# A third place for split weights beside three raw rooms, and a new table of VectorE's taps and modulation steps

## What is computed

```python
mod = c_act @ w_ada[l] + b_ada[l]
shift, scale, gate = jnp.split(mod, 3, axis=-1)
h = _rmsnorm(x, norm_g[l]) * (1.0 + scale[:, None, :]) + shift[:, None, :]
z = h @ w_in[l]
...
y = jnp.concatenate([o_fft, o_na, o_ret, o_cv], axis=-1) @ w_out[l]
x = x + gate[:, None, :] * y
```

## Time and profile before

| what | value |
|---|---|
| time, median of 3 executions | 2083.03 us (2081.29 to 2087.2) |
| the profiled execution's own time | 2087.8 us |
| its span in the profile | 2085.9 us |
| TensorE busy | 2037.2 us, 98% of the span |
| VectorE busy | 1750.0 us, 84% |
| ScalarE busy | 1196.9 us, 57% |
| granted TensorE clock, mean | 0.991 of full |

### The profile page before, as it was taken

The page is one execution under the profiler, slowest core; times in us unless marked ns, Lnnn a source line. Parts: engine busy times, 40 slices in busy tenths (PEclk is TensorE's granted clock), DMA queues, the critical chain, the costliest instruction groups (busy, mean ns, idle before and its releaser), DMA issues.

```text
span 2085.9 us, 42604 instructions
## 1 busy us (share of the span) xinstructions
PE 2037.2 (98%) x18977; PEld 1641.7 (79%) x18977; DVE 1750.0 (84%) x1662; ACT 1196.9 (57%) x1079; POOL 57.0 (3%) x72
## 2 busy tenths in 40 slices
PE   8999999999999999999999999999999999999998
PEld 7889888888889955555556568888888888888887
DVE  7785687998887788999999999989877789898755
ACT  5553644454444578887877864456554454555543
POOL 0002300000000000000000000010000000100000
PEclk9999999999999999999999999999999999999999
DMA  8854577789888878999999987765758776557552
GB/s 302 298 202 165 180 289 271 287 293 329 317 319 300 298 300 343 420 420 420 420 420 413 416 320 277 257 197 190 282 189 302 270 290 245 194 197 275 200 202 102
DMA packets 96742, 595.27 MB, mean 285 GB/s; under 512 B 11176, under 2 KB 11336, under 8 KB 37808
## 3 DMA queue, kind: packets, MB, share of 16 engines
q1 hardware_dynamic: 94912, 583.66, 74.6%
q0 software_dynamic: 1648, 8.90, 1.2%
HBM read 588.32 MB, written 2.10 MB: 283 GB/s over the span
## 4 chain that ended last, share of the span: by engine, by line
PE 73%; DVE 13%; DMA 8%; ACT 3%; issue 2%; DVEq 0%; POOL 0%; ACTq 0%; POOLq 0%
PE GB L2256 54%; PE GB L2685 6%; DVE w_lo L1303 5%; PE MB L2685 4%; DVE W L1303 3%; DMA raw<-w_up 2%; ACT w_hi L653 2%; DMA Z<-w_ada 2%; DMA W<-w_ada 2%; DMA raw<-w_down 1%; DVE W L1274 1%; DMA raw<-w_gate 1%; DVE Z L1274 1%; PE MB L2843 1%; PE MB L2480 1%
## 5 line engine op out<-in xcount | busy, mean ns | idle before, releaser
L653 ACT ACTIVATE w_hi<-raw 128x2048 f16<-128x2048 f32 x308 | 588.1, 1910 | 697.2 <-PE GB L2256 673.6
L1303 DVE SCALAR_TENSOR_TENSOR w_lo<-raw,w_hi 128x2048 f16<-128x2048 f32 x308 | 706.1, 2294 | 236.8 <-ACT w_hi L653 235.5
L2256 PE MATMUL GB<-H,w_hi 128*128 128x256 f16 x4352 | 721.7, 274 | 16.5 <-DVE w_lo L1303 11.6
L2256 PE MATMUL GB<-H,w_lo 128*128 128x256 f16 x2176 | 595.4, 274 | 0.0
L2256 PEld LDWEIGHTS GB<-H,w_hi 128*128 128x128 f16 x4352 | 422.9, 98 | 82.8 <-DVE w_lo L1303 16.3
L2256 PEld LDWEIGHTS GB<-H,w_lo 128*128 128x128 f16 x2176 | 213.7, 98 | 25.4
L1274 DVE SCALAR_TENSOR_TENSOR W<-W,SM 128x1024 f32<-128x1024 f32 x150 | 192.2, 1281 | 35.6 <-DMA W<-w_ada 31.6
L2256 PE MATMUL GB<-w_hi,H 128*128 128x256 f16 x1280 | 210.8, 273 | 0.0
L2256 PE MATMUL GB<-w_lo,H 128*128 128x256 f16 x640 | 174.4, 273 | 0.0
L2256 PE MATMUL GB<-Z,w_hi 128*128 128x256 f16 x1024 | 170.0, 274 | 4.0 <-DVE w_lo L1303 4.0
L2256 PE MATMUL GB<-W,w_hi 128*128 128x256 f16 x1024 | 168.0, 273 | 1.8 <-DVE w_lo L1303 1.8
(11 more groups left out here) (487 smaller groups left out, 2751.2 us busy)
## 6 DMA issues: line engine op xcount, KB each, us to landing
raw<-w_in SPq DMA_DIRECT2D x144, 1024.0 KB, 5.4
W<-w_ada SPq DMA_DIRECT2D x160, 512.0 KB, 5.7
raw<-w_out SPq DMA_DIRECT2D x48, 1024.0 KB, 5.4
raw<-w_down SPq DMA_DIRECT2D x41, 1024.0 KB, 10.3
raw<-w_gate SPq DMA_DIRECT2D x34, 1024.0 KB, 11.7
raw<-w_up SPq DMA_DIRECT2D x32, 1024.0 KB, 12.8
raw<-xattn_wk SPq DMA_DIRECT2D x16, 1024.0 KB, 5.1
raw<-xattn_wq SPq DMA_DIRECT2D x16, 1024.0 KB, 7.6
```

What stands on the lines that cost most here:

```text
L653: act.activation(w, raw_at[r], ACT.Copy, scale=W_SCALE).then_inc(hi_done, 1)
L1303: dve.scalar_tensor_tensor(lo, raw_at[r], W_SCALE, hi, ALU.mult, ALU.subtract).then_inc(raw_taken[r], 1)
L2256: last = pe.matmul(o, a, m, start=first, stop=end and w_part is lo, skip_group_check=True)
```

## The change

Places: `SPL` is 3, and the third place for a high and a low half lies in raw room 3, which the projections no longer load into (three raw rooms). The experts use room 3 as a raw room from their fifth block on, as they keep their own places. `slot` turns the block's number so that the places meet at the borders of the experts' stretch. Waits follow: block m waits for block m - 3, the first expert load into room 3 waits for block 13 of `wo`, and the first block of `z0` waits until the experts gave room 3 up. `load_due(1)` lets the pieces of block m follow the load of block m + 1. The tables `TAPS_AT` and, for `z0` and `z1`, `ada_plan` are new: the sixteen early steps now end after block 11 and not 16, the sixteen late ones stand in pairs after blocks 38 to 42 and 45 to 47. The number of taps and steps is the same.

```diff
--- before.py
+++ after.py
@@ -22,7 +22,7 @@
 BLK = 2048
 RAW = 4
 ROOMS = RAW + 4
-SPL = 2
+SPL = 3
 IN_ORDER = [4, 5, 2, 3, 6, 7, 0, 1, 8, 9]
 POOL_AFTER = 38
 POOL_WINDOWS = (2, 4, 8, 16)
@@ -52,7 +52,7 @@
 GRID_W, NA_KW, NA_KH = 64, 16, 8
 REL_H, REL_W = 2 * NA_KH - 1, 2 * NA_KW - 1
 TAPS = 31
-TAPS_AT = {11: 5, 12: 4, 13: 6, 14: 4, 15: 6, 16: 4, 17: 6, 18: 6, 19: 6, 20: 6, 21: 6, 22: 2, 23: 6, 24: 6, 25: 2, 26: 6, 27: 6, 28: 2, 29: 4, 30: 6, 32: 6, 33: 2, 34: 6, 35: 2, 36: 3, 37: 2}
+TAPS_AT = {11: 5, 12: 6, 13: 6, 14: 6, 15: 6, 16: 6, 17: 6, 18: 6, 19: 6, 20: 6, 21: 2, 22: 6, 23: 6, 24: 2, 25: 5, 26: 6, 27: 2, 28: 1, 29: 6, 31: 6, 33: 6, 34: 1, 35: 5, 36: 4, 37: 3}
 DH = 64
 FOLD, MIRROR = P // 2, T // 2 + 1
 NEG = -1.0e30
@@ -120,9 +120,9 @@
     rooms, uses, last = [], [0] * ROOMS, [-1] * ROOMS
     for b in range(total):
         j = b - first
-        open_ = list(range(RAW))
+        open_ = list(range(RAW - 1))
         if 0 <= j < n:
-            open_ += [4] * (j >= 6) + [5] * (7 <= j < 126) + [6] * (j >= 7) + [7] * (13 <= j < 150)
+            open_ += [3] * (j >= 4) + [4] * (j >= 6) + [5] * (7 <= j < 126) + [6] * (j >= 7) + [7] * (13 <= j < 150)
         r = min(open_, key=lambda r: last[r])
         uses[r], last[r] = uses[r] + 1, b
         rooms.append((r, uses[r]))
@@ -142,9 +142,9 @@
         count[0] += 1
     short = [2, 2, 3, 3, *range(4, 16)]
     def halves(ph):
-        for m in [2, 2, 3, 4, 4, 5, 6, 6, 7, 8, 8, 9, 10, 12, 14, 16]:
+        for m in [2, 2, 3, 4, 4, 5, 6, 6, 7, 8, 8, 9, 9, 10, 10, 11]:
             put(ph, m)
-        for m in [35, 36, 37, 37, 38, 39, 39, 40, 41, 41, 42, 42, 43, 44, 45, 46]:
+        for m in [38, 38, 39, 39, 40, 40, 41, 41, 42, 42, 45, 45, 46, 46, 47, 47]:
             put(ph, m)
     for m in [2 + 2 * k // 3 for k in range(16)]:
         put("w_in", m)
@@ -212,8 +212,8 @@
         bank_free = [S(f"bank_free{j}") for j in range(4)]
 
         raw = sb("raw", [P, RAW, BLK])
-        w_hi = sb("w_hi", [P, SPL, BLK], F16)
-        w_lo = sb("w_lo", [P, SPL, BLK], F16)
+        w_hi = sb("w_hi", [P, 2, BLK], F16)
+        w_lo = sb("w_lo", [P, 2, BLK], F16)
         XT = sb("XT", [P, KC, T])
         H = sb("H", [P, 2 * BLK])
         xh = H[:, 0:BLK].bitcast(F16).rearrange("p (c t) -> p c t", t=T)
@@ -245,6 +245,14 @@
         HID = Zf[:, 8192:8192 + TILES * D_EXP].rearrange("p (k n) -> p k n", n=D_EXP)
         y_hi, y_lo = (Zf[:, k * 1024:(k + 1) * 1024].bitcast(F16).rearrange("p (k n) -> p k n", n=512) for k in range(2))
         hid_at = [H[:, k * 1024:(k + 1) * 1024] for k in range(4)] + [Zf[:, c * T:c * T + 1024] for c in (28, 48)] + [Yf[:, k * 1024:(k + 1) * 1024] for k in range(2)]
+        third = raw[:, RAW - 1, :].bitcast(F16)
+        hi_of = [w_hi[:, 0, :], w_hi[:, 1, :], third[:, 0:BLK]]
+        lo_of = [w_lo[:, 0, :], w_lo[:, 1, :], third[:, BLK:2 * BLK]]
+
+        def slot(s):
+
+            return (s + 2) % SPL
+
         raw_at = [raw[:, r, :] for r in range(RAW)] + [w3, Yf[:, 0:BLK], Yf[:, BLK:2 * BLK], Zf[:, 40 * T:48 * T]]
         hid_t = [a[:, 0:2 * ROWS_SORTED].bitcast(F16).rearrange("p (c n) -> p c n", n=ROWS_SORTED) for a in hid_at]
         slot_index = w2[:, 0:PLACES]
@@ -411,10 +419,10 @@
 
             return 2 + u if i == 0 and ph in K_MAJOR else 4 * i + 2 * u + 1
 
-        def done(eng, ph, j, i=0):
+        def done(eng, ph, j):
 
             s = where(ph, j)[1]
-            eng.wait_ge(block_done[s % SPL], s // SPL + 1 + 2 * i)
+            eng.wait_ge(block_done[s % SPL], s // SPL + 1)
 
         def pieces_in(eng, k):
 
@@ -456,6 +464,8 @@
                 r, n = rooms[where(ph, j)[0]]
                 if n > 1:
                     sp.wait_ge(raw_taken[r], n - 1)
+                elif r == RAW - 1:
+                    done(sp, "wo", 13)
                 elif r == 4:
                     sp.wait_ge(ada_mod, 7)
                 elif r in (5, 6):
@@ -495,7 +505,7 @@
                         m = 4 * k + j
                         load(ph, m, w[2 * n + j % 2, j // 2] if k == 0 and ph in K_MAJOR else w[2 * n + j // 2, j % 2])
                         due.append((ph, plan.get(ph, {}).get(m, [])))
-                        load_due(2)
+                        load_due(1)
                         if beside is not None:
                             beside(m)
 
@@ -636,20 +646,22 @@
                     act.wait_ge(raw_full[r], 16 * n)
                     act.wait_ge(block_done[s % SPL], s // SPL)
                 cut = slice(half * BLK // 2, half * BLK // 2 + BLK // 2)
-                act.activation(w_hi[:, s % SPL, cut], raw_at[r][:, cut], ACT.Copy, scale=W_SCALE).then_inc(hi_done, 1)
+                act.activation(hi_of[slot(s)][:, cut], raw_at[r][:, cut], ACT.Copy, scale=W_SCALE).then_inc(hi_done, 1)
 
             def split(ph, j, i=0):
                 b, s = where(ph, j)
                 r, n = rooms[b]
                 act.wait_ge(raw_full[r], 16 * n)
                 if ph == "moe":
-                    act.wait_ge(block_done[s % SPL], s // SPL - 1)
+                    act.wait_ge(block_done[(s - 4) % SPL], (s - 4) // SPL + 1)
                     if j < 2:
                         act.wait_ge(S("x_o"), 2 * X_HEADS)
                     w = ring_hi[j // 2 % 2][:, j % 2 * BLK:j % 2 * BLK + BLK]
                 else:
-                    act.wait_ge(block_done[s % SPL], s // SPL + 2 * i)
-                    w = w_hi[:, s % SPL, :]
+                    act.wait_ge(block_done[s % SPL], s // SPL)
+                    if (ph, j) == ("z0", 0):
+                        given_up(act, RAW - 1)
+                    w = hi_of[slot(s)]
                 act.activation(w, raw_at[r], ACT.Copy, scale=W_SCALE).then_inc(hi_done, 1)
                 if (ph, j) in parts_due:
                     ada_high(parts_due[ph, j])
@@ -1289,14 +1301,14 @@
                 b, s = where(ph, j)
                 dve.wait_ge(hi_done, s + 1 + half)
                 cut = slice(half * BLK // 2, half * BLK // 2 + BLK // 2)
-                ins = dve.scalar_tensor_tensor(w_lo[:, s % SPL, cut], raw_at[rooms[b][0]][:, cut], W_SCALE, w_hi[:, s % SPL, cut], ALU.mult, ALU.subtract)
+                ins = dve.scalar_tensor_tensor(lo_of[slot(s)][:, cut], raw_at[rooms[b][0]][:, cut], W_SCALE, hi_of[slot(s)][:, cut], ALU.mult, ALU.subtract)
                 if half:
                     ins.then_inc(raw_taken[rooms[b][0]], 1)
 
             def split(ph, j, i=0):
                 b, s = where(ph, j)
                 dve.wait_ge(hi_done, s + 1 + 4 * i + (s > at["z1"][1]))
-                hi, lo = w_hi[:, s % SPL, :], w_lo[:, s % SPL, :]
+                hi, lo = hi_of[slot(s)], lo_of[slot(s)]
                 if ph == "moe":
                     hi, lo = (r[j // 2 % 2][:, j % 2 * BLK:j % 2 * BLK + BLK] for r in (ring_hi, ring_lo))
                 r = rooms[b][0]
@@ -2237,8 +2249,8 @@
             def product(ph, j, b, k0, start, stop, groups=None, x=(xh, xl), rows=False, between=None):
 
                 s = at[ph][1] + j
-                hi = w_hi[:, s % SPL, :].rearrange("p (c n) -> p c n", c=8)
-                lo = w_lo[:, s % SPL, :].rearrange("p (c n) -> p c n", c=8)
+                hi = hi_of[slot(s)].rearrange("p (c n) -> p c n", c=8)
+                lo = lo_of[slot(s)].rearrange("p (c n) -> p c n", c=8)
                 first = start
                 groups = groups or [(range(8), None)]
                 for ks, wait in groups:
```

## The result

| | before | after |
|---|---|---|
| median of the runs side by side, us | 2085.15 (20 runs) | 2089.65 (20 runs) |
| all runs, us | 2079.91 to 2093.94 | 2083.79 to 2095.74 |
| ratio to before | | 1.0024, 95% interval 1.0014 to 1.0034 |
| span of the profiled execution, us | 2085.9 | 2087.1 |
| chance and range given | | same 0.5; 2075 to 2097 |

The change costs 0.24%, some 5 us, and lies in the class within 0.3% that was given the best chance; the forecast said 2087 and a net loss of 4.3. So the figure held. The experiments show that its two halves held too, but that inside the loss two costs were added that don't add, and inside the gain one was put down to the wrong part of the change.

The account below looks back on a forecast made before the run. TensorE, busy 98% of the span, was taken as the bound, standing 49 of 2086 us. Losses of 9.6 less gains of 5.3 make +4.3, so 2087 us on the median's scale; case range 2082 to 2093, overall 2075 to 2097.

Parts of the forecast that it names:

- Gains of the third place: TensorE's waits shrink: wq block 4 by 1.9 us, mix0 blocks 10 and 11 by 1.8, w_in by 0.8.
- The rotation's 0.8 us: In z0 and z1, new taps remove two TensorE waits where the rotation followed a long list: -0.8 us.
- Loss in z0: Packed steps before low halves 10 and 11 cost 2.4 us, later pieces 1.0: +3.4 us.
- Loss in z1: Packed steps 2.4 us plus waiting for pieces make 4.7; less 1.9 of lead: +2.8 us.
- The clock: Waits at block 11 of z0 and z1 bring two falls of 1.7 us: +3.4, ends 0 and 3.4.
- w_in block 3, counted 0: Wait before w_in block 3 follows a list longer than the block, VectorE already late: no gain.
- Edits at nothing: Three raw rooms, other queue depth, first expert load into room 3, z0's first high half: all 0 us.
- A price from a page: Skill page's DMA table gives a 512 KB piece of w_ada 3.2 us, against 5.7 in the trace.
- room shortage: Rival, w_in to mix0: raw loads queue behind waits for steps, TensorE waits; 2092 to 2105 us, chance 0.1.
- The lead: Rival: pieces land in 4.4 us, third place fills before block 9 in both layers; 2074, half 2079; chance 0.22.
- late pairs: Rival: blocks 38 to 42, 45 to 47 wait 1 to 2 us, one fall per layer; +6, 2093; chance 0.08.
- no effect: Rival: third place stays empty almost everywhere, wait for pieces at block 10 hardly grows; 2083 us, chance 0.15.

Follow-up runs that it names:

- the other one with the same early steps: Changed kernel with the late list of steps and the taps put back, packed early steps kept: 2088.94 us, ratio 1.0028 against the kernel before.

## Why the prediction was right, and where it was not

- **The sum.** Forecast +9.6 - 5.3 = +4.3; the medians differ by 4.5, and the parts measured alone are +10.2 and -5.2 (the interval of each is 2 to 3 us either way, so the closeness is in part luck).
- **Gains of the third place: right in sum, not in each.** wq held: the profiles with two places wait there for 0.8 to 1.9 us, those with three for nothing. So did mix0, though this pair of profiles hides it (1.8 to 1.7): with two places it is 1.8 to 3.0 in four profiles, with three 1.7, 1.33 and in seven others nothing. `w_in` did not. Behind block 3 the profile before has 4.1 us and the one after 2.2, but three others with two places have 1.3 to 2.1, and those with three and the same list of steps in `w_in` 0 to 4.2: pieces fall late differently from run to run, and no gain can be read. The forecast's -0.8 is shown by nothing, nor is its 0 for block 11.
- **The rotation's 0.8 us: right, for the wrong part of the change.** They were put down to the new taps. With the new tables and two places both waits stay; with three places and the old tables they are gone. They are the third place's, too small for a ratio to show.
- **Loss in z0: right figure, wrong step.** The forecast was 3.4 us by "2 x 1.2 = 2.4 us, in full on TensorE's path" and 1.0 of waiting for pieces on top. The waits of blocks 9 to 11 grew by 2.9. But the terms are not added: without the pieces 2.79 of the 3.45 us before block 11 stay, without most of the steps' work 3.44 stay.
- **Loss in z1: right in size as far as two profiles tell, the sum behind it not.** Forecast +2.8 of a bound of 4.7. Measured +4.3 in this profile and +1.7 in the other one with the same early steps. The 2.4 of the two steps stood in the sum as work of its own beside the pieces; without pieces no wait is left (0.18), so the work alone costs nothing there and counts only as part of the rooms' time. The waiting for pieces was counted "from the first step of block 8 to the first of block 10"; the second step of block 10 was left out. In this profile it waited longest, 2.82 us, in the other it did not wait.
- **The clock: right.** Two new falls, where they were said to be, +4.0 for the forecast's 3.4. In the other profile with these early steps there was none in z1, and that of z0 cost 3.0. That the falls at w_in 3 and w_out 1 would stay as they were was taken for granted, and was wrong for this profile.
- **w_in block 3, counted 0: right, for a wrong reason.** The text had VectorE late with a long list; ScalarE's high half is what is late.
- **Edits at nothing: right, within 3 us.** Rooms and queue depth 1.0005. Late pairs 1.0028 against 1.0024.
- **A price from a page.** The 3.2 us for a piece rest on a table that the Trainium skill (DMA: Bandwidth & Descriptors, "Anatomy of one DMA — SWDGE (gpsimd) path") gives for a transfer issued by GpSimd. These pieces are issued by SyncE. So the 5.7 of the trace against the 3.2 is no test of that table, and the forecast's sum did not use it.
- **A sign that misled.** "High halves that wait for a raw load would mean the room shortage." They do wait, 48.2 us for w_in alone, but TensorE doesn't: with a third place ScalarE gets so far ahead that the raw block is the next thing it meets. The sign would have had to be a wait of TensorE behind them.
- **The rivals.** The lead did come in wq and mix0, and nowhere near blocks 10 and 11 of z0 and z1. Room shortage, late pairs and no effect are each excluded by a run of their own. The upper end of the room shortage was added up wrongly: 2083 + 4 + 22 is 2109, not 2105.

## What to carry to other kernels

A third place only moves the limit to the next thing that its users wait for: 500 us less waiting on ScalarE was worth 5 us to TensorE. Work that is dealt by one engine's load has a second load, that of the rooms it is fetched through: two rooms where a new piece comes each 6 to 8 us carry no two steps per block of 5.2 us for long, however free VectorE may be. And where two causes stand before the same wait, take each away by itself before adding their prices: in z0 either alone held most of it. Where pieces fall late by chance, read a second profile before a wait's size is explained: here 5.46 and 2.55 us stood at one place with the same steps.

## What was not expected of the hardware

A fall of the granted clock depends on more than how long TensorE stood. In the 13 profiles of this study, the waits at two places that all share, and all others of over 1.6 us before a block of the projections, but for the very first:

| wait, us | times | the clock fell |
|---|---|---|
| w_in 3, 1.93 or 1.94 | 12 | 9 |
| w_out 1, 2.05 or 2.06 | 13 | 5 |
| others, 1.69 to 2.10 | 9 | 1 |
| others, 2.24 to 2.55 | 3 | 0 |
| others, 2.79 to 5.46 | 10 | 10 |

So a wait of 2.8 us or more cost a fall each time, and one of about 2 us did or did not in the same kernel's runs at hand. The length of the wait doesn't decide it alone. In the cross attention nine waits of 2.38 to 2.51 us had a fall each time; in the experts one of 1.85 to 2.07 had it in 4 of 13. And at 797 us of the profile before, the clock fell while TensorE had stood nowhere since 770. Each fall before a block is 1.7 us (2.3 and 3.0 in one each), and the three that differ in the first pair are as large as the whole effect of the change: two single profiles of this kernel can't be compared by their spans. What decides at 2 us stays open. Open as well is how much of the pieces' time (5.2 to 8.2 us from one step to the next in its room, where it was waited for) is their place in the queue behind the raw blocks; no run changed that alone.
